# Third modulation group of layer 0 summed on VectorE during qkv, with its weight chunks loaded ahead of qkv pieces

## The chip, the cores and the metric

One NeuronCore of a Trainium2 chip runs the whole program. The metric is the device time of one execution in microseconds. Three executions of the kernel before took 1296.9, 1297.63 and 1302.68 us; their median, 1297.63 us, is the time before.

## What is computed

The program is a two-layer decoder trunk over 256 tokens of width 1024, all in float32. Each layer begins with a modulation computed from one vector `c`:

```python
cond = jax.nn.silu(c)                       # (1, 1024)
mod = cond @ ada_w[l] + ada_b[l]            # 6*1024 columns: sh1 sc1 g1 sh2 sc2 g2
h = rms_norm(x, norm1_g[l]) * (1.0 + sc1) + sh1
y = dilated_attention(h, ...)               # layer 0: qkv, 16 heads, w_o
x = x + g1 * y
h = rms_norm(x, norm2_g[l]) * (1.0 + sc2) + sh2
x = x + g2 * moe_ffn(h, ...)                # 64 experts, top 6, one shared expert
...
kvmod = cond @ kv_ada_w + kv_ada_b          # shared_kv, before layer 1: shift, scale
```

Layer 1 takes keys and values from `shared_kv`, whose own modulation `kvmod` (1024 x 2048 weights, 8 MB) depends on `c` alone, so it can be computed at any time before layer 1. All expert weights are read once per layer, 3 MB each; they make up most of the 502 MB that the program loads.

## The kernel before, in words

**Tiles and stages.** Layer 0 runs: norm 1 and q in four row blocks of the contraction (PE: `block_sums` L1150, `qkv_block` L1170; VectorE L1924 to L1939); the qkv loop over twelve pieces `c` of 256 columns (0 to 3 are q and come from the row blocks, 4 to 7 are k, 8 to 11 are v; L1219 on PE, L1953 on VectorE, L1486 on ScalarE); attention over eight pairs of heads `g` (L846, L1667, L1399); the output projection `wo` with the residual; norm 2; the experts. Layer 1 follows with the same kind of attention and experts.

**Modulation groups.** A group is 2048 columns of a modulation, read as 8 chunks of 128 x 2048 float32 (1 MB). Group 1 is g1 and sh2 of layer 0, group 2 is sc2 and g2, group 6 is the shared key/value modulation. Groups 0 and 4 have loaders of their own. There are two ways to sum a group's chunks. On VectorE, `ada_step(g, k)` (L1604) multiplies a chunk by column k of `csilu` and adds it to `acc`, and `ada_sums(g)` on PE (L767) then adds up the partitions with 4 matmuls by ones. On PE, `ada_steps(g, k0, k1)` (L782) does the products as 4 matmuls per chunk. Either way the sums stand in PSUM bank 7; ScalarE copies them to `ada_row` (`ada_rows`, L1375), PE turns the row into columns (`ada_columns`, L760), and VectorE adds the bias (`modulation`, L1588). `gate_half` spreads half a gate over the partitions. All of these use bank 7 in turn, kept in order by counters (`ADA_TURN`, `SUMS_TURN`, `GATES_BY`, L404 to L407).

**The ring.** `chunks` is one fixed list (L389); its first 24 are groups 1, 2 and 6. They pass through 5 slots of 1 MB, so chunk i can be loaded only when chunk i-5 has been used (`load_chunks`, L542).

**What orders the work.** Nothing is scheduled at run time. Each engine has its own program with waits on semaphores. SyncE's program (L541) issues nearly all loads into one queue, in an order written out by hand, and a wait of SyncE holds back all loads behind it. `qkv_piece(n)` (L550) loads 512 columns (2 MB) of the qkv weights for the loop pieces 2n and 2n+1. In the qkv loop before, VectorE does the steps of groups 1 and 2 between the normalisations of q and k (`BY_DVE`, L1950); PE sums group 1 after its matmuls of piece 7 and turns it after those of piece 8; PE does group 6 in rounds 2 to 5 of attention, 2 chunks each (L854).

For c below 8 the loop has this exchange, in which ScalarE's next piece starts only after VectorE's reduction of this one:

```python
# VectorE (L1977)                          # ScalarE (L1494)
dve.wait_ge(sem("sq"), c + 1)              act.wait_ge(sem("qkv_ps"), c + 1)
v.tensor_reduce(ssq[:, c, :], ...)         activation(sq[:, c % 2, :], ..., ACT.Square)
ada_step(*next(turns))                     act.wait_ge(sem("ssq"), c + 1)
dve.wait_ge(sem("srt"), c + 1)             activation(srt[:, c, :], ..., ACT.Sqrt)
```

On ScalarE a copy of transposed q or k (`qT`, `kT`, for c from 4) follows in the same piece.

Of the kernel before, what the change touches and what calls it, by code (L numbers as in the profile page):

```python
# [12 lines left out]
ALU = mybir.AluOpType  # L13
# [200 lines left out]
def build(nc: bass.Bass, t: dict, out: bass.AP):  # L214
    with ExitStack() as ctx:
# [50 lines left out]
        with ExitStack() as att:  # L266
# [51 lines left out]
            late_row = kT[:, 4:6, :].rearrange("p h n -> p (h n)")  # L318
        with ExitStack() as moe:
# [86 lines left out]
        SUMS_TURN = {1: 1, 2: 2, 3: 3, 4: 4, 5: 5}  # L406
# [134 lines left out]
        def _(sp):  # L541
# [65 lines left out]
            for l in range(2):  # L607

                if l == 0:
# [9 lines left out]
                    for dst, src in ROWS_B:  # L619
                        sp.dma_start(dst, src).then_inc(sem("rows_b_in"), 16)  # L620
                    qkv_piece(2)
                    sp.wait_ge(sem("qkv_rows_used"), 2)
# [23 lines left out]
                    load_chunks(order[21:number[("wo", 0, 1)] + 1])  # L646
# [82 lines left out]
        def _(pe):  # L729
# [37 lines left out]
            def ada_sums(g):  # L767
# [9 lines left out]
                sums = ada_4[0] if g == 4 else acc  # L777
# [3 lines left out]

            def ada_steps(g, k0, k1):  # L782

                if k0 == 0:
                    pe.wait_ge(sem("mod_sb"), ADA_TURN[g])
                    pe.wait_ge(sem("gate_sb"), GATES_BY[g])
                for k in range(k0, k1):
                    w = use(("ada", g, k))
                    for q in range(4):
                        last = mm(bank[7][32 * q:32 * q + 1, :], csilu[:, k:k + 1], w[:, 0, q * 512:(q + 1) * 512], k == 0,  # L790
                                  k == KT - 1)
                    used(("ada", g, k), last)
# [11 lines left out]
            def attention(l, q_of, k_of):  # L804
# [41 lines left out]
                for g in range(H // 2 + 3):  # L846
                    if g < H // 2:
                        scores(g)
                        if l == 0 and g == 0:
                            ada_columns(2)  # L850
# [3 lines left out]
                        if l == 0 and 2 <= g < 6:  # L854
                            ada_steps(6, 2 * g - 4, 2 * g - 2)
# [363 lines left out]
            for c in range(4, 12):  # L1219
# [108 lines left out]
        def _(act):  # L1328
# [46 lines left out]
            def ada_rows(g):  # L1375
# [3 lines left out]
                if g == 6:  # L1379
                    after(("ada", g, KT - 1))  # L1380
# [16 lines left out]
            def attention(l):  # L1397
                heads, pairs = H * l, H // 2 * l
                for g in range(H // 2 + 3):  # L1399
                    if l == 0 and g == 6:  # L1400
                        ada_rows(6)
# [84 lines left out]
            for c in range(12):  # L1486
                if c == 8:
                    ada_rows(1)
# [21 lines left out]
            ada_rows(2)  # L1510
# [66 lines left out]
        def _(dve):  # L1577
# [26 lines left out]
            def ada_step(g, k):  # L1604

                i = number[("ada", g, k)]
                if k == 0 and g != 1:
                    dve.wait_ge(sem("ada_sums"), SUMS_TURN[g] - 1)
                dve.wait_ge(sem(f"chunk_in{ring_of(i)}"), 16 * (i // RING + 1))
                w = slot(("ada", g, k))[:, 0, :]  # L1610
                if k == 0:
                    ins = v.tensor_scalar(acc[:, :], w, csilu[:, 0:1], None, ALU.mult)
                else:
                    ins = v.scalar_tensor_tensor(out=acc[:, :], in0=w, scalar=csilu[:, k:k + 1], in1=acc[:, :], op0=ALU.mult,  # L1614
# [50 lines left out]
            def attention(l):  # L1665
                heads, pairs = H * l, H // 2 * l
                for g in range(H // 2 + 1):  # L1667
                    if g == 1 and l == 0:
# [256 lines left out]
            for j in range(4):  # L1925
# [13 lines left out]
                last.then_inc(sem("hT_dve"), 1)  # L1939

# [7 lines left out]
            dve.wait_ge(sem("csilu"), 1)  # L1948
            chunks_1_2 = [(g, k) for g in (1, 2) for k in range(KT)]
# [176 lines left out]
```

## Time and profile before

| What | Before |
|---|---|
| median of 3 runs | 1297.63 us |
| span of the profiled execution | 1295.6 us |
| PE busy | 1089.7 us (84%) |
| VectorE busy | 495.4 us (38%) |
| ScalarE busy | 249.3 us (19%) |
| loaded | 502.25 MB, mean 388 GB/s |
| chunk steps on VectorE (L1614) | 28 of 2347 ns each |

The page gives the profiled execution's span, first to last instruction, and not a device time of its own. Its 1295.6 us is 1.3 us under the shortest run (1296.9) and 2.0 us under the median. All times of rows below are microseconds from the start of that span. PE's matmuls are pipelined, so a busy PE is not PE at its peak, and the number of records of a group is not the number of matmuls in the program.

### The profile page before, as it was taken

To read this page: it belongs to the slowest core of one execution; us is meant where nothing else is said; L and a number is where in the kernel's file an instruction comes from. 1 tells how busy PE (TensorE), PEld (TensorE's weight loads), DVE (VectorE), ACT (ScalarE), POOL (GpSimd) and SP (SyncE) were. 2 spreads that over 40 slices of the span, in tenths; PEclk is the share of its full clock that TensorE was granted. 3 is DMA by queue.
4 is the path that set the end of the run, shared out by engine and by line. 5 is a ranking of instruction groups with operands and counts; after the bars stand their busy time and mean duration, and the time that the engine had idled before them with its cause. 6 is when DMAs were issued, how large, how long until landed. Compare 5 with 4: busy or idle time off the path is not lost.

```text
span 1295.6 us, 17378 instructions
## 1 busy us (share of the span) xinstructions
PE 1089.7 (84%) x6680; PEld 605.3 (47%) x6680; DVE 495.4 (38%) x1108; ACT 249.3 (19%) x574; POOL 0.4 (0%) x5
## 2 busy tenths in 40 slices
PE   5999899997887878787768989999878877868886
PEld 4887577543333424342337567745433333423332
DVE  1287874423122123131337877543221313221231
ACT  2121623111011111010122472311100101110110
POOL 0000000000000000000000000000000000000000
PEclk9999999999898999898989999999988999888998
DMA  9999998999999999999989757799999999999996
GB/s 346 389 402 407 367 347 333 383 425 421 424 424 424 422 424 425 422 424 424 424 303 363 298 190 267 288 379 423 423 424 424 423 422 424 422 424 424 425 423 281
DMA packets 101337, 502.25 MB, mean 388 GB/s; under 512 B 12009, under 2 KB 37510, under 8 KB 46982
## 3 DMA queue, kind: packets, MB, share of 16 engines
q1 hardware_dynamic: 100790, 500.92, 95.1%
q8 instruction: 55, 0.90, 0.3%
q10 hardware_dynamic: 464, 0.20, 0.1%
q14 instruction: 28, 0.23, 0.0%
HBM read 500.04 MB, written 1.05 MB: 387 GB/s over the span
## 4 chain that ended last, share of the span: by engine, by line
SPq 52%; PE 31%; DMA 5%; DVE 5%; issue 5%; ACT 2%; DVEq 0%; ACTq 0%
SPq L585 47%; PE bank L739 23%; SPq L684 3%; PE bank L1177 2%; DMA w_dn<-in_moe_w_gate_up 2%; PE bank L742 2%; DMA ring<-in_moe_w_down 1%; SPq L592 1%; PE bank L841 1%; PE bank L983 1%; DMA w_gu<-in_ada_w 1%; ACT p_sb L1412 1%; DMA ring<-in_ada_w 1%; DVE w_dn L1627 1%; PE bank L1158 1%
## 5 line engine op out<-in xcount | busy, mean ns | idle before, releaser
L739 PE MATMUL bank<-w_gu,ring 128*32 128x512 f32 (+1 forms) x1120 | 292.0, 686 | 113.4 <-DMA w_gu<-in_moe_w_gate_up 36.6
L739 PEld LDWEIGHTS bank<-w_gu,ring 128*32 128x32 f32 (+1 forms) x1120 | 77.3, 130 | 279.8 <-issue 279.6
L1844 DVE TENSOR_TENSOR hh<-sg,bank 128x256 f32<-128x256 f32 x44 | 27.3, 621 | 415.7 <-ACT sg L1445 415.7
L739 PE MATMUL bank<-w_gu_x,ring 128*32 128x512 f32 (+1 forms) x352 | 166.9, 687 | 8.1 <-DMA ring<-in_moe_w_gate_up 5.4
L739 PE MATMUL bank<-ring 128*32 128x512 f32 (+1 forms) x272 | 144.6, 682 | 10.1 <-DMA gate<-in_moe_w_gate_up 5.3
L739 PE MATMUL bank<-w_gu,hhT 128*32 128x512 f32 (+1 forms) x416 | 138.1, 596 | 7.4 <-DMA ring<-in_moe_w_down 5.8
L739 PE MATMUL bank<-w_dn,ring 128*32 128x512 f32 x240 | 110.9, 733 | 8.2 <-DMA w_gu_x<-in_moe_w_gate_up 8.2
L1445 ACT ACTIVATE sg<-bank 128x256 f32<-128x256 f32 x44 | 16.9, 384 | 499.2 <-PE bank L739 499.2
L1861 DVE SCALAR_TENSOR_TENSOR bank<-bank,w_slot,gate 128x512 f32<-128x512 f32 x88 | 66.8, 759 | 102.1 <-PE bank L739 102.0
L739 PE MATMUL bank<-ring,hhT 128*32 128x512 f32 (+1 forms) x208 | 87.2, 596 | 0.9 <-DVE hhT L1851 0.6
L739 PE MATMUL bank<-sel,h_hi 128*128 128x256 f32 x352 | 87.8, 290 | 0.0
L739 PE MATMUL bank<-sel,h_lo 128*128 128x256 f32 x352 | 84.2, 279 | 0.0
L1335 ACT ACTIVATE y_hi<-bank 128x512 fp32r<-128x512 f32 x88 | 52.5, 597 | 154.6 <-DVE bank L1861 154.6
L983 PE MATMUL bank<-y_hi,st 128*128 128x512 f32 x176 | 73.6, 418 | 3.1 <-ACT y_hi L1335 3.1
L1335 ACT ACTIVATE ring<-bank 128x512 f32<-128x512 f32 x88 | 47.8, 595 | 146.8 <-PE bank L739 146.8
L983 PE MATMUL bank<-y_lo,st 128*128 128x512 f32 x176 | 69.3, 394 | 0.0
L1614 DVE SCALAR_TENSOR_TENSOR acc<-ring,csilu,acc 128x2048 f32<-128x2048 f32 x28 | 65.7, 2347 | 3.9 <-DMA ring<-in_ada_w 3.6
L739 PEld LDWEIGHTS bank<-sel,h_lo 128*128 128x128 f32 x352 | 66.5, 189 | 0.0
L739 PEld LDWEIGHTS bank<-sel,h_hi 128*128 128x128 f32 x352 | 66.0, 188 | 0.4
L1866 DVE TENSOR_TENSOR y_lo<-bank,y_hi 128x512 fp32r<-128x512 f32 x88 | 60.4, 686 | 3.3
L739 PE MATMUL bank<-xn,hhT 128*32 128x512 f32 (+1 forms) x144 | 58.2, 596 | 0.0
L739 PEld LDWEIGHTS bank<-w_gu,hhT 128*32 128x32 f32 (+1 forms) x416 | 33.9, 119 | 49.6 <-issue 44.7
(299 smaller groups left out, 1677.6 us busy)
## 6 DMA issues: line engine op xcount, KB each, us to landing
w_gu<-in_moe_w_gate_up SPq DMA_DIRECT2D x130, 1024.0 KB, 25.5
w_gu<-in_moe_w_down SPq DMA_DIRECT2D x46, 1024.0 KB, 26.5
w_gu_x<-in_moe_w_gate_up SPq DMA_DIRECT2D x40, 1024.0 KB, 26.0
ring<-in_ada_w SPq DMA_DIRECT2D x36, 1024.0 KB, 10.1
ring<-in_moe_w_gate_up SPq DMA_DIRECT2D x34, 1024.0 KB, 26.3
w_dn<-in_moe_w_gate_up SPq DMA_DIRECT2D x28, 1024.0 KB, 26.4
ring<-in_moe_w_down SPq DMA_DIRECT2D x22, 1024.0 KB, 26.2
w_dn<-in_moe_w_down SPq DMA_DIRECT2D x14, 1024.0 KB, 25.9
```

Of the source, the lines that this page charges most:

```text
L585: sp.dma_start(dst, src).then_inc(sem(f"unit_in{u}"), 16)
L684: index = {j: sp.value_load(tab_i[0:1, j:j + 1], min_val=0, max_val=E - 1) for j in sorted({j for _, j, _ in items if j != "shared"})}
L739: return nc.tensor.matmul(o, a, b, start=first, stop=last)
L742: return nc.tensor.transpose(o, a, const("ident")[0:rows, 0:rows])
L983: last = nc.tensor.matmul(bank[2 * ti + half][:, :], st[:, ti * P:(ti + 1) * P], y[:, half * 512:(half + 1) * 512], start=first and y is y_hi,
L1177: last = nc.tensor.matmul(bank[c][:, ti * N:(ti + 1) * N], hT[:, 2 * j + k, ti * P:(ti + 1) * P], qkv_rows[j][:, k, c * N:(c + 1) * N], st ...
L1335: return nc.scalar.activation(o, i, ACT.Copy, **kw)
L1445: nc.scalar.activation(sg[:, :], bank[b][:, 0:FE], ACT.Silu).then_inc(sem(f"silu_done{l}"), 1)
L1614: ins = v.scalar_tensor_tensor(out=acc[:, :], in0=w, scalar=csilu[:, k:k + 1], in1=acc[:, :], op0=ALU.mult, op1=ALU.add)
L1844: v.tensor_tensor(hh[:, :].rearrange("s (f p) -> s p f", f=FE // P), sg[:, :].rearrange("s (p f) -> s p f", f=FE // P), bank[b][:, FE:2 * ...
L1861: v.scalar_tensor_tensor(out=bank[6 + half][:, :], in0=bank[6 + half][:, :], scalar=w_slot[:, :], in1=gate[:, 1, c], op0=ALU.mult, op1=ALU ...
L1866: v.tensor_tensor(y_lo[:, c], bank[6 + half][:, :], y_hi[:, c].bitcast(F32), ALU.subtract)\
```

## The change

- Group 6 is summed on VectorE, in the qkv loop, after groups 1 and 2. `ada_steps` is gone; PE gets `ada_sums(6)` in round 3 of attention, and its copy on ScalarE comes in round 5 and no longer in round 6.
- Group 2 is summed in a second accumulator, `acc_2`, in the half of `kT` that layer 0 does not use.
- VectorE does six steps of group 1 inside the row blocks, three after block 2 and three after block 3; the other 18 are spread over the loop by `STEPS`.
- SyncE loads chunks 0 to 4 before qkv piece 2, chunks 5 and 6 before piece 3, 7 to 10 before piece 4, 11 to 13 before piece 5, and 14 to 23 right after the gate biases.
- On PE the sum of group 1 moves from piece 7 to 5, its columns from 8 to 6, the gate halves from 9 and 10 to 8 and 9, the sum of group 2 from 11 to 10, its columns from attention's round 0 to piece 11. ScalarE's and VectorE's parts move with them.

```diff
@@ SyncE, layer 0
+                    load_chunks(order[0:1])
+                    sp.wait_ge(sem("ada_0_used"), 1)
+                    load_chunks(order[1:3])
+                    sp.wait_ge(sem("ada_0_used"), 2)
+                    load_chunks(order[3:5])
                     qkv_piece(2)
+                    load_chunks(order[5:7])
                     sp.wait_ge(sem("qkv_rows_used"), 2)
                     qkv_piece(3)
...
-                    load_chunks(order[0:1])
-                    sp.wait_ge(sem("ada_0_used"), 1)
-                    load_chunks(order[1:3])
-                    sp.wait_ge(sem("ada_0_used"), 2)
-                    load_chunks(order[3:5])
+                    load_chunks(order[7:11])
                     sp.wait_ge(sem("qkv_ps"), 4)
                     qkv_piece(4)
-                    load_chunks(order[5:9])
+                    load_chunks(order[11:14])
                     sp.wait_ge(sem("qkv_ps"), 6)
                     qkv_piece(5)
...
+                    load_chunks(order[14:24])
                     sp.wait_ge(sem("xT_ps"), 4)
                     wo_last_load(0)
-                    load_chunks(order[9:21])
@@ PE
-                sums = ada_4[0] if g == 4 else acc
+                sums = ada_4[0] if g == 4 else acc_2 if g == 2 else acc
...
-                        if l == 0 and g == 0:
-                            ada_columns(2)
...
-                        if l == 0 and 2 <= g < 6:
-                            ada_steps(6, 2 * g - 4, 2 * g - 2)
+                        if l == 0 and g == 3:
+                            ada_sums(6)
...
-                if c == 7:
+                if c == 5:
                     ada_sums(1)
-                if c == 8:
+                if c == 6:
                     ada_columns(1)
-                if c in (9, 10):
-                    gate_half(0, c - 9)
+                if c in (8, 9):
+                    gate_half(0, c - 8)
+                if c == 10:
+                    ada_sums(2)
                 if c == 11:
-                    ada_sums(2)
+                    ada_columns(2)
                 qk_transposes(c - 4)
@@ ScalarE
             for c in range(12):
+                if c == 6:
+                    ada_rows(1)
+                if c == 11:
+                    ada_rows(2)
                 if c == 8:
-                    ada_rows(1)
...
@@ VectorE, row blocks
                 last.then_inc(sem("hT_dve"), 1)
+                if j == 2:
+                    dve.wait_ge(sem("csilu"), 1)
+                if j >= 2:
+                    for k in range(3 * j - 6, 3 * j - 3):
+                        ada_step(1, k)
@@ VectorE, qkv loop
-            chunks_1_2 = [(g, k) for g in (1, 2) for k in range(KT)]
-            BY_DVE = {c: chunks_1_2[c:c + 1] for c in range(4)}
-            BY_DVE.update({4: chunks_1_2[4:6], 5: chunks_1_2[6:8]})
-            BY_DVE.update({c: chunks_1_2[2 * c - 6:2 * c - 4] for c in range(7, 11)})
+            chunks_left = iter([(1, 6), (1, 7)] + [(g, k) for g in (2, 6) for k in range(KT)])
+            STEPS = (1, 1, 1, 1, 2, 2, 0, 2, 3, 2, 2, 1)
...
-                if c == 9:
+                if c == 7:
                     modulation(1)
```

## Rows read from the trace of the kernel before

**Rows 1.** The page: span, and the chain that ended last, by engine

```profile
span 1295.6 us, 17378 instructions
...
SPq 52%; PE 31%; DMA 5%; DVE 5%; issue 5%; ACT 2%; DVEq 0%; ACTq 0%
```

**Rows 2.** The chain in order of time, where SyncE's load issues take it over

```profile
283.15 0.04 SPq L585
```

**Rows 3.** Stretches: busy PE, PEld, DVE, ACT, POOL; granted clock, DMA share, GB/s

```profile
40.00:90.00 50.00, 50.00 (x272) 41.82 (x272) 32.33 (x53) 7.06 (x16) 0.00 (x0) 1.00 1.02 398
130.00:150.00 20.00, 17.64 (x165) 8.36 (x164) 17.18 (x74) 13.03 (x52) 0.00 (x0) 1.00 0.92 365
250.00:650.00 400.00, 323.18 (x2012) 147.12 (x2004) 102.64 (x192) 49.54 (x93) 0.00 (x0) 0.94 1.01 424
```

**Rows 4.** SyncE's queue in order of time: start, length, line, transfer

```profile
28.62 4.29 SPq L616 DMA_DIRECT2D w_gu<-in_a_w_qkv  x1
...
36.48 0.39 SPq L551 DMA_DIRECT2D w_dn<-in_a_w_qkv  x1
42.32 0.39 SPq L551 DMA_DIRECT2D w_gu<-in_a_w_qkv  x1
...
44.09 0.64 SPq L626 DMA_DIRECT2D pos_q<-in_pos  x1
```

**Rows 5.** Issues of those four: count, KB each, us from issue to landing

```profile
w_gu<-in_a_w_qkv SPq DMA_DIRECT2D x1, 1024.0 KB, 12.8
...
w_dn<-in_a_w_qkv SPq DMA_DIRECT2D x1, 2048.0 KB, 10.3
...
w_gu<-in_a_w_qkv SPq DMA_DIRECT2D x1, 2048.0 KB, 10.1
...
pos_q<-in_pos SPq DMA_DIRECT2D x1, 1.0 KB, 11.4
```

**Rows 6.** VectorE in order of time, end of the row blocks and qkv

```profile
50.33 0.16 DVE L1928 TENSOR_TENSOR mod<-bank,vcol 128x4 f32<-128x4 f32 x1 [8.44 <-PE bank L739]
...
62.93 0.67 DVE L1978 TENSOR_REDUCE ssq<-sq 128x8 f32<-128x512 f32 x1
63.52 2.34 DVE L1614 SCALAR_TENSOR_TENSOR acc<-ring,csilu,acc 128x2048 f32<-128x2048 f32 x1
...
66.74 0.68 DVE L1978 TENSOR_REDUCE ssq<-sq 128x8 f32<-128x512 f32 x1
```

**Rows 7.** ScalarE in order of time, pieces 6 and 7 of the qkv loop

```profile
90.55 0.30 ACT L1499 ACTIVATE srt<-ssq,cst 128x8 f32<-128x8 f32 x1 [7.91 <-DVE ssq L1978]
90.76 0.67 ACT L1335 ACTIVATE qT<-bank,qk_gain 128x512 f32<-128x512 f32 x1
...
93.44 0.59 ACT L1335 ACTIVATE ada_row<-bank 128x512 f32<-128x512 f32 x1
```

**Rows 8.** TensorE in order of time, qkv loop and attention

```profile
81.28 7.07 PE L739 MATMUL bank<-w_gu,hT 128*128 128x256 f32 x32
88.28 1.04 PE L739 MATMUL bank<-acc,cst 128*1 128x512 f32 x8
...
96.65 0.95 PE L739 MATMUL bank<-cst,ada_row 128*128 128x4 f32 x8
...
123.77 0.93 PE L739 MATMUL bank<-kT,qT 64*128 64x128 f32 x8 [0.78 <-ACT kT L1335]
...
132.41 1.90 PE L739 MATMUL bank<-ring,csilu 128*1 128x512 f32 x16 [1.22 <-issue]
```

**Rows 9.** VectorE in layer 0's attention, first operation of a round

```profile
140.31 1.02 DVE L1686 SCALAR_TENSOR_TENSOR s_sb<-negrel,bank 128x384 f32<-128x384 f32 x2 [0.64 <-PE bank L739]
...
154.07 1.02 DVE L1686 SCALAR_TENSOR_TENSOR s_sb<-negrel,bank 128x384 f32<-128x384 f32 x2 [1.23 <-PE bank L739]
```

**Rows 10.** Stretches around a wait of TensorE, columns as in rows 3

```profile
319.00:324.00 5.00, 0.00 (x0) 0.00 (x0) 4.89 (x7) 0.60 (x1) 0.00 (x0) 0.99 1.02 426
324.00:331.00 7.00, 6.18 (x32) 1.61 (x32) 0.53 (x2) 0.00 (x0) 0.00 (x0) 0.52 1.01 425
```

More of the change, by code:

```diff
@@ L318, in build @@
             late_row = kT[:, 4:6, :].rearrange("p h n -> p (h n)")
+            acc_2 = kT[:, 8:16, :].rearrange("p h n -> p (h n)")
         with ExitStack() as moe:
@@ L405, in build @@
         AMP_TURN = {1: 5, 2: 7, 3: 8}
-        SUMS_TURN = {1: 1, 2: 2, 3: 3, 4: 4, 5: 5}
+        SUMS_TURN = {1: 1, 2: 2, 6: 3, 3: 4, 4: 5, 5: 6}
         GATES_BY = {1: 0, 2: 2, 6: 4, 4: 4, 3: 4, 5: 6}
@@ L645, in _ @@
                     fixed_loads(0, EARLY_UNITS[2:4])
-                    load_chunks(order[21:number[("wo", 0, 1)] + 1])
+                    load_chunks(order[24:number[("wo", 0, 1)] + 1])
                     sp.wait_ge(sem("qkv_ps"), 10)
@@ L780, in ada_sums @@
                 last.then_inc(sem("ada_sums"), 1)
[L782 to L792, printed above, removed]
             def gate_half(n, half, b=7):
@@ L1378, in ada_rows @@
                     act.wait_ge(sem("ada_sums"), SUMS_TURN[g])
-                if g == 6:
-                    after(("ada", g, KT - 1))
                 copy(row_of[g][:, :], bank[7][:, :]).then_inc(sem("row_sb"), 1)
@@ L1399, in attention @@
                 for g in range(H // 2 + 3):
-                    if l == 0 and g == 6:
+                    if l == 0 and g == 5:
                         ada_rows(6)
@@ L1509, in _ @@
                         copy(kT[:, 2 * b - 8:2 * b - 6, :].rearrange("p k n -> p (k n)"), src).then_inc(sem("qkT_sb"), 1)
-            ada_rows(2)
             attention(0)
@@ L1606, in ada_step @@
                 i = number[("ada", g, k)]
-                if k == 0 and g != 1:
+                if k == 0 and g == 2:
+                    dve.wait_ge(sem("ada_0_used"), 4)
+                elif k == 0 and g == 6:
+                    dve.wait_ge(sem("ada_sums"), SUMS_TURN[1])
+                elif k == 0 and g != 1:
                     dve.wait_ge(sem("ada_sums"), SUMS_TURN[g] - 1)
@@ L1610, in ada_step @@
                 w = slot(("ada", g, k))[:, 0, :]
+                sums = acc_2 if g == 2 else acc
                 if k == 0:
-                    ins = v.tensor_scalar(acc[:, :], w, csilu[:, 0:1], None, ALU.mult)
+                    ins = v.tensor_scalar(sums[:, :], w, csilu[:, 0:1], None, ALU.mult)
                 else:
-                    ins = v.scalar_tensor_tensor(out=acc[:, :], in0=w, scalar=csilu[:, k:k + 1], in1=acc[:, :], op0=ALU.mult,
+                    ins = v.scalar_tensor_tensor(out=sums[:, :], in0=w, scalar=csilu[:, k:k + 1], in1=sums[:, :], op0=ALU.mult,
                                                  op1=ALU.add)
@@ L1667, in attention @@
                 for g in range(H // 2 + 1):
-                    if g == 1 and l == 0:
+                    if g == 0 and l == 0:
                         modulation(2, 1, 32, col("norm2_g", 0, 8))
@@ L1947, in _ @@
                                            in1=col("kv_k_norm", rows=HD), op0=ALU.mult, op1=ALU.mult))
-            dve.wait_ge(sem("csilu"), 1)
-            chunks_1_2 = [(g, k) for g in (1, 2) for k in range(KT)]
-            BY_DVE = {c: chunks_1_2[c:c + 1] for c in range(4)}
-            BY_DVE.update({4: chunks_1_2[4:6], 5: chunks_1_2[6:8]})
-            BY_DVE.update({c: chunks_1_2[2 * c - 6:2 * c - 4] for c in range(7, 11)})
+            chunks_left = iter([(1, 6), (1, 7)] + [(g, k) for g in (2, 6) for k in range(KT)])
+            STEPS = (1, 1, 1, 1, 2, 2, 0, 2, 3, 2, 2, 1)
             for c in range(12):
-                turns = iter(BY_DVE.get(c, ()))
-                if c == 9:
+                turns = iter([next(chunks_left) for _ in range(STEPS[c])])
+                if c == 7:
                     modulation(1)
-                if c in (10, 11):
-                    gate_half(0, c - 10)
+                if c in (9, 10):
+                    gate_half(0, c - 9)
                 if c == 6:
@@ L1979, in _ @@
                         .then_inc(sem("ssq"), 1)
-                    if c < 6:
+                    if STEPS[c]:
                         ada_step(*next(turns))
```

## The prediction, made before the changed kernel was run

> **What bounds the kernel now.** Read first the chain that ended last: over half of the span is SyncE's queue, about a third is PE [rows 1]. In order of time the two do not mix. After the start-up the chain is PE with few gaps until 283 us, where SyncE's load issues take it over [rows 2]. The stretches say why: from 250 us on the DMA engines move 424 GB/s without a pause, while PE has room [rows 3]. So the 283 us before are a head during which PE sets the pace, and the experts follow at DMA's pace. A microsecond won or lost on PE in qkv or attention of layer 0 moves everything behind it, since the loads of the experts wait for buffers that PE empties; I take it to reach the end in full. But DMA is not idle in the head: from 40 to 90 us its share is 1.02 at 398 GB/s [rows 3]. Loads can't come sooner there, they can only change places.
>
> **What the change takes from PE.** Attention's rounds 2 to 5 each hold matmuls for two chunks, 1.9 us a round in the record, 1.8 up to the next instruction [rows 8]. In their place stands one sum, 1.0 us. In rounds 4 to 6 VectorE waits 0.63 us a round for PE, and 1.23 us before round 7 [rows 9]; without PE's steps VectorE's own work sets the round. That is 3 x 0.63 + 1.23 = 3.1 us at most, less VectorE's modulation of group 6 (two operations of 0.16 each, by the mod operation of [rows 6]) and what the new sum and its copy (0.59 [rows 7]) disturb: I take **2.2 us** off. The bounds are 0 and 3.1 us.
>
> A rule speaks even against this. The Trainium skill ("Perfetto Trace Analysis", Identifying the Most-Contended Engine) says that matmul busy time is no good measure of PE's headroom and that the share of LDWEIGHTS is better. From 130 to 150 us LDWEIGHTS is busy 8.36 of 20 us, VectorE 17.18 [rows 3]; by that rule PE is not the engine to relieve, and attention would give nothing. VectorE's repeated wait for PE speaks against the rule.
>
> **What it adds, and where: the order of the loads.** Eight steps of 2.34 us [rows 6] go to VectorE. The steps are not the trouble, their chunks are. The last row block of qkv weights is issued at 28.62 and lands 12.8 later, at 41.4; piece 2 at 36.48 + 10.3 = 46.8, piece 3 at 42.32 + 10.1 = 52.4, the last of the small mask loads at 44.09 + 11.4 = 55.5 [rows 4, 5]. Back to back, then: 5.5 us for a piece, 3.1 for the mask loads, and 1.05 MB / 424 GB/s = 2.5 us for a chunk [rows 3]. I lay the new order on this from 41.4: chunks 0 to 4 land at 43.9, 46.4, 48.9, 51.4, 53.9; piece 2 at 59.4; chunks 5, 6 at 61.9, 64.4; piece 3 and masks at 73.0; chunks 7 to 10 from 75.5 to 83.0; piece 4 at 88.5; chunks 11 to 13 at 91.0, 93.5, 96.0; piece 5 and gate biases (1 MB) at 104; chunks 14 to 23 from 106.5 to 129. A check by bytes: up to chunk 11 it is 18.7 MiB = 19.6 MB, at 398 GB/s 49.3 us, so 90.7. SyncE is held by ring slots (chunk 5 waits for chunk 0's use, and so on), but the queue always has some loads ahead, so that costs nothing.
>
> Now VectorE and PE, step by step.
> - Row block 2: VectorE takes chunk 2 at 48.9, ends at 51.3, and only then does block 3's modulation and scaling, which began at 50.33 [rows 6]. PE has matmuls of the block before until about 51.9 (an estimate: eight of the 32 that take 7.1 us in [rows 8]); the scaled block comes at 52.7: **0.8 us** lost.
> - Before the loop: chunk 5 lands at 61.9, its step ends at 64.2; then about 0.9 us of small operations (an estimate: five of the length of the mod operation and their gaps) and the first piece, 3.8 us (62.93 to 66.74) [rows 6], ready at 68.9. PE comes for it at about 67: **1.8 us** lost.
> - PE's sum of group 1, now after piece 5, needs chunk 7's step: 75.5 + 2.3 = 77.8; PE comes at 76.1: **1.7 us** lost.
> - PE's columns of group 1 after piece 6 are the large one. They need ScalarE's `ada_rows(1)`, and ScalarE reaches it only when its piece 5 is done: the square root waits for VectorE's `ssq(5)`, and VectorE does that only after both steps of its piece 4, the second of which takes **chunk 11**. So 91.0 + 2.3 = 93.3, the reduction 0.6, the square root 0.3, the copy of q 0.6, the row copy 0.6 [rows 6, 7]: 95.4. PE has ended piece 6 at 81.3 - 0.5 (its transposes) + 0.8 + 1.8 + 1.7 + 1.0 (the moved sum [rows 8]) = 86.1. **9.3 us** lost. Behind this wait stand all further matmuls of qkv; DMA has no work that would profit.
>
> The first three only set when PE comes to the fourth wait, not when it leaves it, so I count in place and not as a sum of losses: PE begins piece 7 at 95.4 + 0.8 (columns) + 0.4 (transposes) = 96.6, where it began at 81.28: 15.3 later. From there to the first scores (123.77 [rows 8]) PE no longer has the sum and the columns of group 1 (1.0 + 0.8, to the next instruction) and gains the columns of group 2 (0.85): **14.4 us later**, at 138.2. VectorE does not hold that up again: chunk 23 lands at 129, the value copy of piece 11 comes behind PE's matmuls at 136, the last step ends at 138.5, the scores at 139.1. So the late chunk 23, which would have cost time on the old schedule, hides in PE's delay.
>
> **The clock.** PE stood still for over 5 us up to 324 us; its granted clock from 324 to 331 was 0.52, the 1.2 GHz level, after 0.99 in the wait [rows 10]. After a wait of 9 us I expect the same for part of such a stretch: matmuls at half rate for 2 x 2 us cost **2 us**. From no low stretch behind the wait to the whole 7 us of the row, it is 0 to 3.5.
>
> **Sum.** 14.4 - 2.2 + 2.0 = 14.2 us: span 1309.8. The profiled execution's span lies 2.0 under the median of the runs shown, so **1311.8 us** to compare with 1297.63. For a measurement of this kernel 0.5% (6.5 us) is about what can be told from no change.
>
> **Range of the likeliest.** Low: landings 1.5 us earlier (as if qkv pieces too moved at 424 GB/s), no clock, the full 3.1: 1297.6 + 14.4 - 1.5 - 3.1 = 1307. High: landings 3 us late (as much as the small mask loads took, so loads need not be even), clock 3.5, attention 0: 1297.6 + 14.4 + 3 + 3.5 = 1318.5.
>
> **Rivals.**
> - *It pays as meant, and PE's whole saving counts:* group 6 costs PE 4 x 1.8 = 7.2 less 1.0 = 6.2 us less, no chunk is late, 1291.4. Against it: DMA at 1.02 share, which gives chunk 11 no earlier place than behind three pieces. It decides if chunk 11 lands before 82 us. A weaker form, VectorE's bound of 2.2, gives 1295.4. Chance 0.10 together; the strong form stands at the edge of 0.5%, and I put half of the chance beyond it.
> - *Only the last chunk bites:* if ScalarE's order does not hold PE at group 1's columns, VectorE still can't end chunk 23's step before 129 + 2.3 = 131.4, where its attention work began once the first scores were there, at 123.77 + 0.93 = 124.7 [rows 8]; 6.7 - 2.2 = 4.5, 1302.1. For it: nothing but that I could have misread ScalarE's order; the wait on `ssq(5)` stands in its program. Chance 0.13.
> - *Attention gives nothing* (the rule above, worked out here as VectorE and ScalarE setting the rounds at their old pace): 14.4 + 2.0, 1314.0. Chance 0.12.
> - *The stall is absorbed later*, because DMA catches up while PE stands: every load behind chunk 28 waits for a slot or unit that VectorE or PE frees after attention, and DMA already idles in the head (0.92 share at 130 to 150 [rows 3]), so it gains nothing by waiting. If half were absorbed, 1305. Chance 0.08.
>
> The forecast has 0.57. The range that leaves out 2 in 10 reaches from 1302 to 1319. Faster by over 0.5%: 0.05 (the first rival's strong form). Within 0.5%: 0.18 (its weak form and the second rival). Slower by over 0.5%: 0.77.
>
> **What would show it.** In the changed profile: the `ada_row` columns on PE after piece 6 with an idle of 8 to 10 us before them, put down to ScalarE; ScalarE's square root before that waiting for `ssq`; VectorE's step of chunk 11 waiting for DMA until about 91; the granted clock low right behind the wait; first scores at about 138 to 141; attention's rounds at 3.7 to 3.8 us; the first SyncE piece of the chain at about 297. I am wrong if chunk 11 lands well before 88, if PE's idle there is short, or if the first scores are late and SyncE's takeover still stands at 283.

## The result, and the profile after

| What | Before | After |
|---|---|---|
| median, 4 runs of each side by side | 1297.79 us | 1314.48 us (1313.17 to 1317.89) |
| ratio, 95% interval | | 1.0114 [1.0088, 1.014] |
| span of the profiled execution | 1295.6 us | 1313.2 us |
| VectorE busy | 495.4 us | 512.7 us |
| mean granted clock | 0.950 | 0.940 |

The kernel is 1.1% slower, 16.7 us by the medians; predicted were 14.2 us and 1311.8. The page, span, busy time and the chain by engine:

```profile
span 1313.2 us, 17284 instructions
...
PE 1097.8 (84%) x6624; PEld 612.3 (47%) x6624; DVE 512.7 (39%) x1116; ACT 250.2 (19%) x574; POOL 0.4 (0%) x5
...
SPq 54%; PE 26%; DMA 6%; DVE 6%; issue 5%; ACT 2%; DVEq 0%; ACTq 0%
```

PE's share of the chain fell from 31 to 26% [rows 1], DMA's and VectorE's rose by a point each. That looks like relief for PE and is the opposite: PE waits. The chain in order of time shows for whom (start, length, what):

```profile
68.22 21.23 DMA ring<-in_ada_w
...
89.48 2.36 DVE kT L1610
...
91.86 0.70 DVE ssq L1976
...
92.79 0.67 ACT qT L1326
93.46 0.50 ACT ada_row L1326
...
94.00 1.87 PE bank L742 x8
...
170.74 1.28 PE bank L832 x5
...
297.67 0.04 SPq L586
```

A chunk in transfer (chunk 11; it lands at 89.45), its step, the reduction `ssq(5)`, the square root (92.58), q's copy, the row's copy, and then PE's columns: link for link the path that the prediction gave for chunk 11. The two last rows are the first product of the output projection (156.21 in the same view of before, by L841) and SyncE's takeover (283.15 in [rows 2]): both 14.5 us later. PE in order of time, with the idle time before and what ended it:

```profile
69.21 0.66 PE L745 MATMUL bank<-cst,qkn 128*128 128x128 f32 x4 [1.86 <-DVE qkn L1984]
...
94.00 1.87 PE L742 MATMUL bank<-cst,ada_row 128*128 128x4 f32 x8 [8.76 <-ACT ada_row L1326]
95.73 1.09 PE L745 MATMUL bank<-cst,qkn 128*128 128x128 f32 x4
96.62 8.64 PE L742 MATMUL bank<-w_gu,hT 128*128 128x256 f32 x32
...
139.53 1.58 PE L742 MATMUL bank<-kT,qT 64*128 64x128 f32 x16 [0.78 <-ACT kT L1326]
...
161.48 0.89 PE L745 MATMUL bank<-cst,p_sb 128*128 128x128 f32 x6 [1.80 <-ACT pT_sb L1326]
...
169.04 0.89 PE L745 MATMUL bank<-cst,p_sb 128*128 128x128 f32 x6 [1.43 <-ACT pT_sb L1326]
```

Against [rows 8]: piece 7 begins at 96.62 where it began at 81.28, and takes 8.64 us; the later pieces take 7.07. The first scores come at 139.53, 15.8 later. VectorE in order of time:

```profile
61.94 2.35 DVE L1610 SCALAR_TENSOR_TENSOR acc<-ring,csilu,acc 128x2048 f32<-128x2048 f32 x1 [4.45 <-DMA ring<-in_ada_w]
...
74.15 2.35 DVE L1610 SCALAR_TENSOR_TENSOR acc<-ring,csilu,acc 128x2048 f32<-128x2048 f32 x1 [4.40 <-DMA ring<-in_ada_w]
...
89.48 2.35 DVE L1610 SCALAR_TENSOR_TENSOR kT<-ring,csilu,kT 128x2048 f32<-128x2048 f32 x1 [1.63 <-DMA ring<-in_ada_w]
...
137.58 0.69 DVE L1989 COPY v_sb<-bank 128x512 f32<-128x512 f32 x1 [3.20 <-PE bank L742]
138.19 2.34 DVE L1610 SCALAR_TENSOR_TENSOR acc<-ring,csilu,acc 128x2048 f32<-128x2048 f32 x1
```

VectorE stands three times for a chunk (5, 7, 11) behind a 2 MB piece of qkv. The stretches behind the wait and in attention (columns as in [rows 3]; the clock is the seventh, 0.50 is the 1.2 GHz level):

```profile
90.00:97.00 7.00, 3.00 (x13) 2.96 (x14) 6.90 (x6) 1.85 (x4) 0.00 (x0) 0.50 1.02 395
97.00:104.00 7.00, 7.00 (x27) 5.92 (x26) 5.37 (x18) 0.88 (x2) 0.00 (x0) 0.80 1.04 418
130.00:150.00 20.00, 16.63 (x98) 11.70 (x98) 16.35 (x44) 6.71 (x20) 0.00 (x0) 0.94 1.02 406
```

The first matmuls of the output projection on PE, before and after:

```profile
156.14 3.72 PE L841 MATMUL bank<-ring,hT 128*128 128x256 f32 x16
```

```profile
170.67 3.72 PE L832 MATMUL bank<-ring,hT 128*128 128x256 f32 x16
```

**Where the time came from.** First scores +15.8; from there to the output projection 31.1 us against 32.4, so attention gives 1.2 back and leaves +14.5; the experts' loads of layer 0 run 14.5 late at every equal count of bytes; another 3 come in layer 1's head, in which no instruction was changed, and +17.6 reaches the end.

### The profile page after: what moved, and what is told of

Same layout as the page of the kernel before. It is cut to its first block, busy times and chain, and to the rows that moved or that the text cites. A ratio compares the mean times of both kernels' runs of the same rounds, so it can differ in the third digit from the quotient of the medians.

```text
span 1313.2 us, 17284 instructions
## 1 busy us (share of the span) xinstructions
PE 1097.8 (84%) x6624; PEld 612.3 (47%) x6624; DVE 512.7 (39%) x1116; ACT 250.2 (19%) x574; POOL 0.4 (0%) x5
## 4 chain that ended last, share of the span: by engine, by line
SPq 54%; PE 26%; DMA 6%; DVE 6%; issue 5%; ACT 2%; DVEq 0%; ACTq 0%
SPq L586 46%; PE bank L742 22%; DMA ring<-in_ada_w 3%; SPq L687 3%; DMA ring<-in_moe_w_down 3%; SPq L593 2%; PE bank L745 2%; SPq L617 1%; PE bank L832 1%; SPq L615 1%; PE bank L972 1%; ACT p_sb L1401 1%; DVE s_sb L1688 1%; PE bank L895 1%; DVE acc L1610 1%
## 5 line engine op out<-in xcount | busy, mean ns | idle before, releaser
L742 PE MATMUL bank<-w_gu,ring 128*32 128x512 f32 (+1 forms) x1120 | 295.9, 699 | 111.1 <-DMA w_gu<-in_moe_w_gate_up 36.3
L742 PE MATMUL bank<-w_gu_x,ring 128*32 128x512 f32 (+1 forms) x352 | 164.0, 678 | 8.0 <-DMA ring<-in_moe_w_gate_up 5.3
## 6 DMA issues: line engine op xcount, KB each, us to landing
ring<-in_ada_w SPq DMA_DIRECT2D x36, 1024.0 KB, 11.6
```

The source lines that it names most:

```text
L742: return nc.tensor.matmul(o, a, b, start=first, stop=last)
```

## The experiments

"After" and "before" are the two kernels. The "wait for the row" is PE's idle time ahead of group 1's columns, 8.76 us in after. Spans are those of profiled executions, one each, and so are all times of rows.

One thing varies between these executions ahead of every changed instruction: the start-up. The granted clock from 20 to 30 us was 0.83 or 0.84 in ten of the twelve and 1.00 in two (PE relieved in attention, and the first mixed version), where PE came to its last row block at 47 us and not at 49 to 50. Where VectorE waits for chunk 2 there, this is evened out (the qkv loop begins at 60.02 to 60.18 in after and the five kernels built on it); in the kernels built on before it is not, and moves all times up to the scores by up to 2 us.

### Taking the named wait away: the row's copy moved up

On after, ScalarE copies group 1's row before it waits for `ssq(5)`.

```diff
@@ ScalarE, qkv loop, on after
-                if c == 6:
-                    ada_rows(1)
...
                     nc.scalar.activation(sq[...], bank[...], ACT.Square)
+                    if c == 5:
+                        ada_rows(1)
                     act.wait_ge(sem("ssq"), c + 1)
```

> The changed kernel with one thing moved: ScalarE copies the sums of group 1 inside its piece 5, behind the square and ahead of its wait for VectorE's reduction, and no longer at the start of piece 6. PE's wait ahead of the columns of group 1 (8.8 us in the changed kernel) should fall to about 2 us in any theory. Theory A (two limits of nearly the same size: behind the row copy stands VectorE, late by its chunks and its eight more steps): the wait comes back at piece 9, where PE's second gate half waits about 6.5 us for VectorE's first; first scores at 137 to 139.5 (139.5 in the changed kernel), total 1310 to 1314. Theory B (the row copy's place in ScalarE's program is the whole cost, as the prediction had it): first scores at about 131 to 133, total about 1304 to 1307.

Measured: 1319.44 us, ratio to before 1.0154 [1.0126, 1.0183]. PE in order of time:

```profile
86.59 1.05 PE L742 MATMUL bank<-cst,ada_row 128*128 128x4 f32 x8 [1.38 <-ACT ada_row L1326]
...
87.98 8.76 PE L742 MATMUL bank<-w_gu,hT 128*128 128x256 f32 x32
...
118.09 2.05 PE L742 MATMUL bank<-ada_row,cst 128*128 128x512 f32 x2 [5.80 <-DVE gate L1593]
...
139.11 1.58 PE L742 MATMUL bank<-kT,qT 64*128 64x128 f32 x16 [0.78 <-ACT kT L1326]
```

The wait for the row goes, 7.4 us, and comes back as 5.80 us three pieces later, where PE needs bank 7 and VectorE's `gate` operation stands behind chunk steps. The first scores come 0.4 us sooner, as the first theory had it; the 1.2 GHz level returns behind the new wait (0.50 from 116 to 122 us) and takes part of the rest. So there are two limits of nearly the same size: the landing of chunk 11, and the sum of 24 steps with their waits on VectorE. The total is above the line expected, 1310 to 1314: the clock is low again at 163 to 170 and 208 to 214 us, and the experts' loads run 19.1 us late.

### Taking the second limit away: group 6 back on PE, alone and with the first

```diff
@@ PE, attention, on after (ScalarE's copy of the row back to round 6)
-                        if l == 0 and g == 3:
-                            ada_sums(6)
+                        if l == 0 and 2 <= g < 6:
+                            ada_steps(6, 2 * g - 4, 2 * g - 2)
@@ VectorE
-            STEPS = (1, 1, 1, 1, 2, 2, 0, 2, 3, 2, 2, 1)
+            STEPS = (1, 1, 1, 1, 2, 2, 0, 2, 0, 0, 0, 0)
```

> The changed kernel with group 6 back on PE in attention's rounds 2 to 5, so that VectorE does 16 steps and not 24; the order of loads and all the rest stay. Theory A and the prediction's fourth step: the wait of about 8.8 us ahead of the columns of group 1 stays, because it hangs on chunk 11 of group 2; first scores at about 139.5, attention as long as before, total 1315 to 1317. Rival (VectorE's eight more steps are the cost): first scores near 125 to 130, total 1298 to 1304.

And the same with the row's copy moved up:

> Both edits at once: the early row copy and group 6 back on PE. Theory A: both limits are lifted, what is left is the order of the loads (small waits for chunks 5, 7 and VectorE's first steps); first scores at 132 to 134, attention as before, total 1305 to 1308. If the two were additive and independent, this would be the sum of the effects of the two single runs; theory A says that it is much more than that sum, since each alone gives about nothing.

Measured: 1329.11 us, 1.0231 [1.0203, 1.026], and with both edits 1319.02 us, 1.0162 [1.0136, 1.0188]. PE, group 6 on PE alone:

```profile
93.89 1.87 PE L742 MATMUL bank<-cst,ada_row 128*128 128x4 f32 x8 [8.81 <-ACT ada_row L1338]
...
139.31 1.58 PE L742 MATMUL bank<-kT,qT 64*128 64x128 f32 x16 [0.78 <-ACT kT L1338]
...
182.76 6.38 PE L844 MATMUL bank<-ring,hT 128*128 128x256 f32 x16 [7.23 <-issue]
```

PE, with both edits:

```profile
86.38 1.06 PE L742 MATMUL bank<-cst,ada_row 128*128 128x4 f32 x8 [1.32 <-ACT ada_row L1338]
...
130.80 1.58 PE L742 MATMUL bank<-kT,qT 64*128 64x128 f32 x16 [0.78 <-ACT kT L1338]
...
173.95 5.22 PE L844 MATMUL bank<-ring,hT 128*128 128x256 f32 x16 [8.35 <-issue]
```

The first scores, in four cells: after 139.53; the row's copy early 139.11; eight steps less 139.31; both 130.80. Neither limit alone is worth anything, both together 8.7 us.

The totals miss what was expected (1315 to 1317 and 1305 to 1308) for another reason, which I had not seen when I wrote the expectations: L844, the output projection, stands for 7.23 and 8.35 us. The profile names no releaser ("issue"); that it waits for its weights is read from SyncE's program and tested below. SyncE in order of time, group 6 on PE alone:

```profile
92.75 61.29 SPq L549 DMA_DIRECT2D ring<-in_kv_ada_w  x8
154.09 0.44 SPq L560 DMA_DIRECT2D xn<-in_a_w_o  x1
```

With PE using group 6's chunks only in attention, chunk 21 waits for the slot of chunk 16 until about 150 us (SyncE's longest wait for PE there is 37.3 us). In after's order 14 to 23 stand in one row, so SyncE waits there and holds the weights of the output projection and the first experts behind it. Before issued chunks 21 to 23 later, behind the first expert loads.

### Both edits, with the loads in a fitting order

```diff
@@ SyncE, on the kernel with both edits
-                    load_chunks(order[14:24])
+                    load_chunks(order[14:21])
...
-                    load_chunks(order[24:number[("wo", 0, 1)] + 1])
+                    load_chunks(order[21:number[("wo", 0, 1)] + 1])
```

> x5_both with one edit of SyncE: chunks 21 to 23 loaded behind the first expert loads, as in the kernel before, and not ahead of the last wo columns. In x5 and x2 PE releases the slots of group 6 only in attention, SyncE stands at chunk 21 with all other loads behind it, and PE later waits for a wo chunk (8.35 us in x5). Theory A: first scores as in x5, 130.8; no such wait; all of the delay behind the first scores is gone, so the loads of the experts run about 7.0 to 8.5 us behind the kernel before and the total is 1305 to 1307. Rival (the order of the loads alone costs nothing, and x5's 20.7 us were something else than SyncE's stand): the wait before the output projection stays, total near 1317.

Measured: 1309.81 us, 1.0082 [1.0054, 1.0111]; 9.2 us less than with both edits alone, but 3 above the line expected. PE:

```profile
87.89 7.07 PE L742 MATMUL bank<-w_gu,hT 128*128 128x256 f32 x32
...
130.93 1.58 PE L742 MATMUL bank<-kT,qT 64*128 64x128 f32 x16 [0.78 <-ACT kT L1338]
...
166.28 3.72 PE L844 MATMUL bank<-ring,hT 128*128 128x256 f32 x16
```

The wait is gone. From first scores to output projection it takes 35.4 us, where before takes 32.4: the first product of group 6 waits 3.88 us for chunks and gates, and the clock is low at 137 to 144. Experts' loads stand at +11.6. The first scores are still 7.2 later than before. 6.1 of that have names: the qkv loop begins 0.9 late (60.03 for 59.14), then PE waits 1.83 for VectorE's `qkn`, 1.37 at the row, 0.91 for VectorE's `mod` and 0.27 for its `gate`, and the columns of group 2, 0.85, now stand ahead of the scores.

### The clock by itself: PE kept busy in the wait

On after, 17 multiplications into a bank that is free at that point stand ahead of group 1's columns.

```diff
@@ PE, qkv loop, on after
                 if c == 6:
+                    pe.wait_ge(sem("qkT_sb"), 1)
+                    for i in range(17):
+                        mm(bank[4][:, 0:N], hT[:, 0, 0:P], w[:, 0, :], True, True)
                     ada_columns(1)
```

> The changed kernel with 17 matmuls of no use (results in a free bank) ahead of the columns of group 1, about 7.4 us of PE work that ends before the row is there, so that PE does not stand still. The granted clock should stay at 1.00 from 86 to 104 us, the matmuls of piece 7 take 6.9 to 7.1 us and not 8.4 to 8.6, the columns and transposes their old length. The clock as the prediction priced it: 2 to 3.5 us less, first scores at about 136.5, total 1310.5 to 1313. Rival (the low clock lies inside the wait and costs nothing, or the added matmuls delay what follows): no gain or a loss.

Measured: 1313.93 us, 1.0131 [1.0098, 1.0163]; not told apart from after. PE, then the stretch behind the wait:

```profile
85.56 7.61 PE L742 MATMUL bank<-w_gu,hT 128*128 128x256 f32 x34 [0.38 <-ACT qT L1329]
93.93 1.05 PE L742 MATMUL bank<-cst,ada_row 128*128 128x4 f32 x8 [0.77 <-ACT ada_row L1329]
...
137.06 1.58 PE L742 MATMUL bank<-kT,qT 64*128 64x128 f32 x16 [0.78 <-ACT kT L1329]
```

```profile
90.00:97.00 7.00, 6.23 (x35) 5.34 (x34) 6.90 (x6) 1.85 (x4) 0.00 (x0) 1.00 1.02 394
```

The clock stays at 2.4 GHz, the row comes at the same time, and the first scores come 2.5 us sooner than in after. That is the price of the low clock, of which I had put down 2; right behind piece 7 it is 2.9 (102.66 for 105.53). It does not last: attention takes 31.7 us in place of 31.1, a low stretch from 206 to 210 us in the router takes back about 1.5, and the experts' loads are 14.2 us late, in after 14.5. The Trainium skill ("TensorE: Matmul & The Clock Gate", HAM oscillation — how this bites in real kernels) says that PE must be kept from idling to keep its clock. These two stretches agree, 1.00 with work in the wait and 0.50 without. But it is not the length of a wait alone that decides here: with the row early, piece 7 took 8.76 us behind a wait of 1.38 us, its clock 0.53 and 0.62 from 88 to 92 us; with both edits it was the same behind 1.32 us; and with the loads in a fitting order, on the same program up to that point, it took 7.07 behind 1.37 us. What decides between these is open.

### The delay by itself: before, with PE held up by as much

34 multiplications after piece 6 of the kernel before, 14.6 us of PE's time, and nothing else.

```diff
@@ PE, qkv loop, on before
                 last.then_inc(sem("qkv_ps"), 1)
+                if c == 6:
+                    pe.wait_ge(sem("qkT_sb"), 1)
+                    for i in range(34):
+                        mm(bank[4][:, 0:N], hT[:, 0, 0:P], w[:, 0, :], True, True)
```

> The kernel before with nothing but 34 matmuls of no use on PE after piece 6 of the qkv loop, 14.6 us of PE work without a stand. It asks what a delay of PE in qkv is worth at the end. Theory A: the whole delay reaches the experts (their loads 14.6 us later, less about 1 us if a wait of PE later in qkv hides in it), total 1311.5 to 1313. Rival 1 (the experts, bound by DMA, absorb some): total below 1308. The changed kernel was 17.6 us later at the end but 14.5 in layer 0's experts; the missing 3 us came in layer 1's head where nothing was changed. Rival 2: a shift by itself costs those 3 us there (the granted clock falls otherwise), total 1314 to 1316.

Measured: 1316.29 us, 1.0123 [1.0086, 1.0159]. PE, and below it the chain where SyncE takes over:

```profile
138.47 0.93 PE L739 MATMUL bank<-kT,qT 64*128 64x128 f32 x8 [0.78 <-ACT kT L1339]
```

```profile
300.42 0.04 SPq L585
```

+14.7 at the first scores, +17.2 in the experts of layer 0, +20.8 at the end of the profiled execution, whose time of 1318.20 us is above the median. Nothing of a delay of PE in qkv is absorbed; with the loads, the ring and VectorE's steps of before it alone makes the slowdown. The theory put down first, 1311.5 to 1313, is too low; the time lies with the second rival, a shift that also changes where the clock falls. The extra beyond 14.7 stands where the clock is low: 1.0 in attention (at 166 to 172 us), 1.5 in the router (208 to 212), and 3.7 in layer 1's head.

### What attention gives: before, with PE's group 6 work nearly gone

Each chunk of group 6 gets one matmul of 4 columns in place of 4 of 512. This leaves out most of the shared key/value modulation.

```diff
@@ PE, ada_steps, on before
-                    for q in range(4):
-                        last = mm(bank[7][32 * q:32 * q + 1, :], csilu[:, k:k + 1], w[:, 0, q * 512:(q + 1) * 512], ...)
+                    last = mm(bank[7][0:1, 0:4], csilu[:, k:k + 1], w[:, 0, 0:4], k == 0, k == KT - 1)
```

> The kernel before with the products of group 6 left out on PE but for 4 columns of one matmul per chunk (the shared key/value modulation is wrong by that, and with it layer 1's data). It asks what PE's work for group 6 costs in attention, with no price paid elsewhere. Theory A (VectorE bounds the rounds without it): the start of the output projection's first matmuls, 156.2 before, comes 1.5 to 3 us earlier, the total 1295 to 1297. Rival (PE's saving counts in full): 6 to 7 us earlier, total about 1291. Layer 1's routing differs, so the time up to layer 0's experts is the one to read.

Measured: 1302.66 us (10 runs), 1.0021 [1.0, 1.0042] against 1298.32 (24 runs); neither theory's time. From layer 1 on the program works on other data, so only the part up to layer 0's experts can be compared. PE in attention, then the stretch of [rows 3]:

```profile
136.03 1.51 PE L742 MATMUL bank<-cst,p_sb 128*128 128x128 f32 x6 [2.68 <-ACT pT_sb L1333]
...
156.75 3.50 PE L839 MATMUL bank<-ring,hT 128*128 128x256 f32 x15
```

```profile
130.00:150.00 20.00, 12.58 (x110) 9.04 (x108) 16.59 (x73) 12.31 (x48) 0.00 (x0) 0.83 0.97 365
```

PE is busy 12.58 of these 20 us in place of 17.64 [rows 3], and the output projection still begins at 156.75, where it began at 156.14. The first scores came at 122.63, 1.1 us early, by the start-up alone (the qkv loop began at 57.00 for 59.14), so attention took 34.1 us in place of 32.4. The clock is 0.83 in this stretch and was 1.00: with less to do PE ran part of it at 1.2 GHz (at 136.03 the six matmuls of a round take 1.51 us; in after, at 161.48, 0.89). So leaving out PE's products did not shorten attention. This does not say that they cost nothing: at the high clock one of VectorE's rounds takes 3.58 us (140.65 to 144.23) where before has 4.30 (140.31 to 144.61), and its waits of 2.35 and 2.83 us for PE, at the low clock, take that back.

### Looking for a version that beats both

On before: four early steps on VectorE (two after block 2, two after block 3), four chunks ahead of piece 2, the second accumulator, five chunks of group 6 on VectorE and three on PE in rounds 2 to 4, rows and columns in their old places.

```diff
@@ VectorE, on before
-            chunks_1_2 = [(g, k) for g in (1, 2) for k in range(KT)]
...
+            chunks_left = iter([(1, k) for k in range(4, KT)] + [(2, k) for k in range(KT)] + [(6, k) for k in range(5)])
+            STEPS = (1, 1, 1, 1, 2, 1, 0, 2, 2, 2, 2, 2)
@@ PE, attention
-                            ada_steps(6, 2 * g - 4, 2 * g - 2)
+                            ada_steps(6, g + 3, g + 4)
...
```

> A version meant to beat both, built on the kernel before. Four chunks are loaded ahead of piece 2 and four steps done in the row blocks (two after block 2, two after block 3, so no chunk is waited for there); group 2 has the second accumulator; sums, columns and gates of groups 1 and 2 keep their old places; VectorE takes five chunks of group 6 and PE the last three, one a round in rounds 2 to 4, and the sum of VectorE's part in round 5. Theory A (each chunk lands before VectorE comes to it, by the landing times measured in the changed kernel): first scores at 123.8 to 124.5, attention 1 to 2.5 us shorter, the output projection at about 154.5, total 1295 to 1297. Rival (a chunk is late somewhere, or the clock falls when PE has more gaps): no gain, 1298 to 1300.

Measured: 1305.35 us (12 runs), 1.0047 [1.0028, 1.0065], above the theory and the rival. The first scores come at 122.93, 0.8 early, but the qkv loop had begun 1.5 early (57.63 for 59.14) by the start-up, so this version lost 0.7 in it. PE then stands for chunk 21, which in the old order is issued behind the expert loads:

```profile
135.35 1.89 PE L743 MATMUL bank<-ring,csilu 128*1 128x512 f32 x8 [4.97 <-DMA ring<-in_kv_ada_w]
```

So chunks 21 to 23 were put right behind chunk 20; the kernel before ran beside it as one more variant, unchanged, to show how far two sets of runs of the same kernel lie apart:

```diff
@@ SyncE, on the version above
-                    load_chunks(order[15:21])
+                    load_chunks(order[15:24])
```

> x7_hybrid with one edit of SyncE: chunks 21 to 23 loaded right behind chunk 20 and ahead of the last wo columns and the first expert loads. In x7 PE stood 4.97 us in round 2 for chunk 21, which lay behind four expert loads. Expected: no such wait, first scores at 122.9 as in x7, start of the output projection's matmuls 2.5 to 4 us earlier than x7's 158.7, so 155 to 156.5 beside 156.1 in the kernel before. By x3 (PE's products left out, and yet nothing won) relieving PE in attention brings nothing that lasts, because the granted clock falls when PE has gaps there: total 1298 to 1303, not below the kernel before. Rival (x7 lost only by its late chunk): total 1294 to 1297, better than before.

> The kernel before once more, for a second profile of the same program. Its runs spread from 1295.8 to 1305.9. Theory (the spread is where the granted clock falls): if this execution is one above 1299, the profile shows more stretches of low granted clock in layer 1's head (660 to 850 us) or in layer 0's norm 2 and router (190 to 215 us) than the first profile, which has almost none there, and the time is lost in just those stretches; if it is one near 1296, they look like the first. Rival (the spread is DMA's): the expert loads between 300 and 650 us run at a lower rate in a slow one.

Measured: 1303.12 us (12 runs), 1.0028 [1.0013, 1.0043] against 1300.43 (23 runs); before again 1301.9 (8 runs), 1.0012 [0.9992, 1.0032]. PE, the version above:

```profile
123.51 0.93 PE L743 MATMUL bank<-kT,qT 64*128 64x128 f32 x8 [0.78 <-ACT kT L1344]
...
149.74 1.87 PE L743 MATMUL bank<-cst,ada_row 128*128 128x4 f32 x8 [2.05 <-ACT ada_row L1344]
...
157.79 2.43 PE L850 MATMUL bank<-ring,hT 128*128 128x256 f32 x10
```

No wait for a chunk or for VectorE is left in qkv, the scores are 0.3 early (0.2 of it from the start-up), PE has 1.04 in place of 1.90 us of group 6 in a round, and attention takes 34.3 us in place of 32.4: the clock is low from 126 to 133 and again from 150 to 156, and the columns, 1.06 before, take 1.87. The first of these stretches is no mark of this version: it stands in before too, up to 130, and in before again up to 133, where attention takes 32.9. The output projection, expected at 155 to 156.5, begins at 157.79. Nothing here beats the kernel before.

The question put to before again stays open: its profiled execution took 1298.12 us and looks like the first from 655 us on (clock 0.98), so no slow execution of this kernel was profiled.

## Why the prediction was right, and where it was off

**The sign, the path and the place are right.** Chunk 11's landing holds VectorE's step, that `ssq(5)`, that ScalarE's row, that PE. Each link was on record, and the signs named are there: 8.76 us idle put down to ScalarE, for 9.3; chunk 11's step waiting until 89.48, for about 91; clock 0.50 behind it; first scores at 139.53, for 138 to 141; two rounds of attention from 161.48 to 169.04, 3.78 us each, for 3.7 to 3.8; the takeover at 297.67, for about 297.

**The landings.** Chunks 0 to 6 and piece 2 came within 0.1 us of the list made by hand. Piece 3 with the masks took 7.3 us in place of 8.6, so that from there all was early: chunk 11 at 89.45 for 91.0, chunk 23 at 127.3 for 129. The term mis-sized is above all the 3.1 us of the small mask loads: 2.1 measured.

**The small losses.** The loop begins 1.0 late (60.18 for 59.14), for 0.8. In this execution 0.7 of it came from the start-up (the columns ahead of row block 3 stand at 50.01 for 49.34) and 0.4 from the block; with both edits, where the start-up was that of before (49.24), the block lost 1.0. The next wait was 1.86 for 1.8. The third, 1.7 at the sum of group 1, did not come: chunk 7's step ended at 76.5, as PE came. PE was at the row's wait at 85.2, not 86.1. The row came at 94.0, not 95.4, and the two errors nearly cancel in the wait.

**The clock.** 2 us put down, 2.5 measured by keeping PE busy. Piece 7 began at 96.62, the very number predicted, and that was luck: the row was 1.4 early, and the columns and transposes took 2.6 for 1.2, most of it because they ran at 1.2 GHz (1.4 with PE kept busy). First scores without a clock term at 138.2, with it at 140.2; measured 139.53.

**"VectorE does not hold that up again" was wrong as a reason.** It is true while PE is 15 us late. It hid a second limit: with the first away VectorE's `gate` costs 5.80, and only both edits bring 8.7 us. The last step, which I had end at 138.5, ended at 140.5, since its value copy had to wait for PE until 137.58, and attention began 0.4 late.

**Attention: 2.2 predicted, 1.2 measured.** The bounds 0 to 3.1 held. VectorE's rounds 3 to 7 took 19.88 us (148.06 to 167.94) in place of 21.84 (132.23 to 154.07), a gain of 2.0 in the place named; the start, 0.4 late, and the way from the last round to the output projection took some back. But 1.2 is one execution against one: attention took 31.1, 31.7 and 33.2 us in three kernels with group 6 on VectorE (after, PE kept busy, the row early) and 32.4, 32.9 and 33.4 in three with it on PE (before twice, the delay alone). The rule weighed there, that LDWEIGHTS and not matmul busy time tells whether PE has room (the Trainium skill, "Perfetto Trace Analysis", Identifying the Most-Contended Engine), forecast the outcome of two of the runs: PE relieved on the kernel before gained nothing (156.75 for 156.14), and the mixed version took 34.3 us. Whether its reason holds here no run shows. At the high clock the relieved rounds were 0.7 shorter (3.58 for 4.30), as VectorE's repeated wait had said; what was won there was lost where the clock was low.

**Carried in full to the end: right up to layer 1, short behind it.** 14.5 at the output projection, 14.5 at the takeover, 17.6 at the end. The last 3.1 were in no term. They go with the clock of layer 1's head. The stretch of 220 us around it, before and after:

```profile
655.00:875.00 220.00, 200.45 (x1179) 138.16 (x1179) 139.38 (x362) 78.67 (x207) 0.00 (x0) 0.98 0.77 294
```

```profile
670.00:890.00 220.00, 201.57 (x1168) 140.10 (x1168) 138.83 (x361) 78.63 (x206) 0.00 (x0) 0.96 0.76 289
```

The same 64 matmuls, before and after:

```profile
683.14 10.64 PE L739 MATMUL bank<-ring,qT 128*128 128x256 f32 x64 [2.16 <-issue]
```

```profile
696.76 12.32 PE L742 MATMUL bank<-ring,qT 128*128 128x256 f32 x64 [2.07 <-issue]
```

After is 13.6 us behind at their start and 15.3 at their end. Two more groups of equal matmuls take longer in the same way, 1.5 us at 772 to 777 in attention and 1.6 at 826 to 831 behind the output projection (5.46 us for 3.84); a wait for VectorE that is shorter in after gives 1.2 back, and at 831.31 it is 17.6 behind.

Over the eleven profiled executions beside the first of before, the time added between 240 and 340 MB loaded and the clock of this stretch go together. Six with a clock of 0.95 or 0.96 added 2.9 to 4.0 us (after, the row early, group 6 on PE, the delay alone, PE relieved, the first mixed version); five with 0.98 or 0.99 added between -0.9 and +0.1. In after the slower matmuls, 1.7 + 1.5 + 1.6 us, less the 1.2 given back and 0.9 won ahead of them, where the clock was low in before itself, account for the 3 us; that the same holds for the other five is argued from this agreement (PE relieved has other data there), and no run changed the clock of this stretch by itself. What decides on which side an execution falls is open: kernels with the same instructions there fell on both, and I have one profile of each.

**The rivals.** Only the last chunk (1302.1) and "pays as meant" fall with the first scores at 139.53. "Absorbed later" falls with the delay alone, which came through in full. "Attention gives nothing", 1314.0, is nearest to the number by chance: attention gave 1.2, and the head of layer 1 took 3. No run moved chunk 11's load alone: that its landing sets the row's time is read from the chain and from VectorE's wait of 1.63 us for it. That the row hung on ScalarE's place behind `ssq(5)` is shown by the run with the row early.

## What to carry to other kernels

When a queue is already full, moving loads ahead delays others by their bytes: write the new landing times down one by one and follow each late one through every engine's program order to whoever waits, since that gave this result to within 3 us. After naming the limit, ask for the next one on the same stretch: here two of equal size lay over each other, and an edit to either alone won nothing. Work taken from PE was not all won here, because its clock then stood lower (0.79 to 0.90 over attention in the six executions with PE relieved in whole or in part, 0.90 to 0.95 in before twice and the delay alone), and in an in-order load queue a reused slot has to be free by the time its load comes up, or everything behind it is late.

## What the runs showed that I had not expected

- PE's clock fell without a long wait. In the kernel with PE relieved the longest wait in attention is 2.68 us, and the clock from 130 to 150 us is 0.83 where before has 1.00; behind waits of 1.3 to 1.4 us in qkv it fell in two executions and not in a third. The Trainium skill ("TensorE: Matmul & The Clock Gate", A second HAM failure mode: psum-queue depth-cycling) tells of a clock that swings when PE idles briefly and often between groups of matmuls; this stretch agrees.
- A local gain or loss on PE does not keep its size. 2.5 us won by keeping PE busy were 0.3 in the experts; 14.7 us of delay were 17.2 there and 20.8 at the end.
- The kernel before is itself spread over 1295.82 to 1305.92 us in 62 runs, with a median of 1300.0. The 28 runs under 1299 us have a mean clock of 0.9495, the 24 over 1301.5 one of 0.9459. With 12 runs against 23 the interval was 0.15% or 2 us to each side, so a difference of 3 us needs about a dozen runs on each side (an estimate).
